# Two decoder blocks on one core: norms, scale, turning and splitting by row tile at the experts' end, and turnings placed among early products

## The chip, the cores and the metric

The kernel runs on one core of one Trainium2 chip. The metric is the device time of one execution in microseconds (us), given as the median of several runs; smaller is better. The matrix engine is PE (TensorE), the elementwise engines are DVE (VectorE), ACT (ScalarE) and POOL (GpSimd), and SP (SyncE) issues most DMAs. PE's clock has two levels, 2.4 GHz (granted clock 1.00 in the profile) and 1.2 GHz (0.50).

## The reference, cut to what matters

Two blocks of a language model work one after the other on 512 tokens of width 1024, all in float32.

```python
for l in range(2):                                    # block one
    p = x @ w_in[l]                                   # four mixers follow
    h = layer_norm(ALPHA * h + mix, ln1_g, ln1_b)
    f = swiglu(h, ...) if l == 0 else moe(h, ...)     # 8 experts, top 2
    h = layer_norm(ALPHA * h + f, ln2_g[l], ln2_b[l])
# block two: x is block one's h
x = x + 0.5 * rms_norm(swiglu(rms_norm(x, ffn1_pre_g), ...), ffn1_post_g)
y = hybrid_mixer(rms_norm(x, mix_pre_g), ...)
x = x + rms_norm(y, mix_post_g)
x = x + 0.5 * rms_norm(swiglu(rms_norm(x, ffn2_pre_g), ...), ffn2_post_g)
```

Between block one's experts and block two's first feed-forward stand a layer norm, a root-mean-square norm with the gain `ffn1_pre_g`, and nothing else.

## The kernel before

Tokens are four row tiles (t = 0 to 3) of 128 tokens; features are eight tiles of 128. A float32 product is made of three products of rounded parts: every operand is split into a rounded part (ACT copies it) and a rest (DVE subtracts), so one "unit" of a feed-forward (128 gate and 128 up columns for 512 tokens) is 48 matmuls of 512 columns, and a projection piece of 256 columns is 48 as well. The layer's input must lie with features on the partitions, in `XR` (`x_split`): PE transposes it ("turns" it) into PSUM, ACT copies the rounded part, DVE subtracts for the rest.

The program is a row of stages, each a `Block` in which every engine has its own list of instructions; all engines meet at a stage's end. Inside, engines wait only for semaphore counts. The order on each engine is the order in which it is written.

- **Start.** `stage_load` (L2688 to L2704) loads the input `x` in one DMA, then constants, then the first two weight pieces, and waits for the inputs. `stage_to_feature` (L2725 to L2744) turns all 32 tiles, ACT and DVE split them by feature tile. `stage_stream` then splits piece 0 (ACT L2864, DVE L2884) and multiplies (PE L2847).
- **Experts.** `stage_moe` loops over eight experts. Its DVE function `end` (L3881, L3887) adds the last expert rows, which POOL gathers by indirect DMA (L3712) after ACT has stored them. Then come five stages: `stage_layer_norm` (DVE L3289 to L3301, ACT's early rounding of the next gate/up unit L219), `stage_begin_two` (a copy, L3907), `stage_pre_norm` (ACT squares L3944, L3949, DVE L3957), `stage_to_feature` (PE L2725, ACT L2733, DVE L2744, and the rest of the early unit, DVE L225), `stage_ffn` (PE L2506 to L2508).
- **Ends of other stages.** A tail (`MixOut`, `LayerTail`, `RootTail`, `OutTail`) norms row tile by row tile, and PE turns each tile (`pe_turn`; L2194 in `MixOut`, L1784 in the others). As soon as tiles 0 and 1 are split, a `HeadStart` lets PE multiply the next stage's first unit or piece for those 256 tokens (`pe_first_tokens`, L242, 48 matmuls of 256 columns); the next stage opens with the other 256 tokens (`pe_last_tokens`, L242 too). In `MixOut` and `LayerTail` all 48 stand ahead of the turning of tile 3; in `RootTail` and `OutTail` tile 2 is turned first, then come the 48, then tile 3.

## Time and profile before

| what | us |
|---|---|
| median of 3 runs (2971.95 to 2977.4) | 2974.25 |
| the profiled execution | 2977.13 |
| its span, first to last instruction | 2975.3 |
| PE busy | 2775.5 (93%) |
| DVE busy | 1543.2 (52%) |
| ACT busy | 1086.0 (37%) |
| POOL busy | 208.2 (7%) |

The span is 1.8 us shorter than the execution; the rest lies before the first and after the last instruction. PE is the busiest engine by far. A matmul's printed time overlaps with its neighbours' (512 columns are printed as 390 ns and follow each other every 227 ns), so the starts of rows are the better ruler. "Idle before" in a row is the time for which the engine had nothing to do, and what ended it.

### The profile page before, as it was taken

What the parts mean: (1) busy time and instruction counts of PE and PEld (TensorE: products, weight loads), DVE (VectorE), ACT (ScalarE), POOL (GpSimd) and SP (SyncE); (2) the same over time, 40 slices, a digit from 0 to 9 for tenths busy, and PEclk for the clock granted to TensorE, in tenths of its full rate; (3) what the DMA queues carried; (4) which work ended last, traced back from release to release, by engine and by line L of the source; (5) the groups of instructions that cost most, each with busy time, mean ns of one, the idle gap of its engine ahead of it and who ended that gap; (6) DMA issues with size and microseconds to landing.
All of it is one profiled execution on the core that took longest, in us unless ns stands there. A gap on an engine that the chain in (4) does not pass through costs nothing. (4 is left out here: it accounts for less than half of the span.)

```text
span 2975.3 us, 38798 instructions
## 1 busy us (share of the span) xinstructions
PE 2775.5 (93%) x14972; PEld 2386.3 (80%) x14972; DVE 1543.2 (52%) x2136; ACT 1086.0 (37%) x1524; POOL 208.2 (7%) x205
## 2 busy tenths in 40 slices
PE   7999999999999999969999999949999997899999
PEld 5778888888877798858988888848888775788887
DVE  3526675233355366647777777773232525742433
ACT  2434223222233242235555565532232416531222
POOL 0011200000000122050000000110000002000000
PEclk9998889999999999979999999979999996899999
DMA  4210024143222100248888888954242120251521
GB/s 152 90 62 1 29 71 124 50 138 85 85 83 90 45 1 29 86 123 235 250 237 234 228 236 235 271 144 113 60 135 85 54 64 20 85 142 50 149 69 66
DMA packets 435566, 335.25 MB, mean 113 GB/s; under 512 B 23488, under 2 KB 375744, under 8 KB 435312
## 3 DMA queue, kind: packets, MB, share of 16 engines
q1 hardware_dynamic: 429360, 318.14, 37.2%
q0 software_dynamic: 3008, 10.09, 1.0%
q10 hardware_dynamic: 3072, 5.24, 0.5%
q8 instruction: 91, 1.49, 0.2%
q14 instruction: 35, 0.29, 0.0%
HBM read 323.43 MB, written 9.99 MB: 112 GB/s over the span
## 5 line engine op out<-in xcount | busy, mean ns | idle before, releaser
L2506 PE MATMUL psum<-x_split,gate_up_split 128*128 128x512 f32 x1024 | 399.2, 390 | 2.1 <-PEq L2715 2.1
L2507 PE MATMUL psum<-x_split,gate_up_split 128*128 128x512 f32 x1024 | 399.0, 390 | 0.0
L2508 PE MATMUL psum<-x_split,gate_up_split 128*128 128x512 f32 x1024 | 398.9, 390 | 0.0
L3586 PE MATMUL psum<-x_slots_split,gate_up_split 128*128 128x320 f32 x1424 | 381.1, 346 | 16.4 <-DVE gate_up_split L3807 12.9
L3587 PE MATMUL psum<-x_slots_split,gate_up_split 128*128 128x160 f32 x1424 | 315.9, 242 | 0.0
L2634 DVE TENSOR_TENSOR arena<-arena,psum 128x512 f32<-128x512 f32 x66 | 45.4, 688 | 488.1 <-ACT arena L2572 488.1
L2847 PE MATMUL psum<-x_split,w_split 128*128 128x512 f32 x1152 | 271.9, 395 | 12.0 <-DVE w_split L2884 6.8
L3586 PEld LDWEIGHTS psum<-x_slots_split,gate_up_split 128*128 128x128 f32 x1424 | 262.6, 190 | 24.6 <-issue 22.6
L2847 PEld LDWEIGHTS psum<-x_split,w_split 128*128 128x128 f32 x1152 | 217.0, 190 | 66.6 <-issue 14.5
L3587 PEld LDWEIGHTS psum<-x_slots_split,gate_up_split 128*128 128x128 f32 x1424 | 266.1, 192 | 1.9
L2572 ACT ACTIVATE arena<-psum 128x512 f32<-128x512 f32 x66 | 39.6, 601 | 594.9 <-PE psum L2508 594.9
L2506 PEld LDWEIGHTS psum<-x_split,gate_up_split 128*128 128x128 f32 x1024 | 192.5, 188 | 42.3 <-issue 2.3
L2508 PEld LDWEIGHTS psum<-x_split,gate_up_split 128*128 128x128 f32 x1024 | 192.6, 188 | 40.1
L2507 PEld LDWEIGHTS psum<-x_split,gate_up_split 128*128 128x128 f32 x1024 | 192.6, 188 | 39.8
L3807 DVE TENSOR_TENSOR gate_up_split<-arena,gate_up_split 128x2048 fp32r<-128x2048 f32 x88 | 201.0, 2284 | 0.0
L2602 DVE TENSOR_TENSOR gate_up_split<-arena,gate_up_split 128x2048 fp32r<-128x2048 f32 x63 | 144.4, 2292 | 75.9 <-ACT gate_up_split L2553 75.9
L2525 PE MATMUL psum<-down_split,hidden_split 128*128 128x512 f32 x432 | 168.6, 390 | 1.1 <-DVE hidden_split L2636 1.1
L2526 PE MATMUL psum<-down_split,hidden_split 128*128 128x512 f32 x432 | 168.1, 389 | 0.0
L2527 PE MATMUL psum<-down_split,hidden_split 128*128 128x512 f32 x432 | 168.1, 389 | 0.0
L3740 ACT ACTIVATE gate_up_split<-arena 128x2048 fp32r<-128x2048 f32 x88 | 167.4, 1903 | 0.0
L3812 DVE TENSOR_TENSOR down_split<-arena,down_split 128x512 fp32r<-128x512 f32 x176 | 121.2, 692 | 70.6 <-ACT down_split L3746 70.0
L2847 PE MATMUL psum<-w_split,x_split 128*128 128x512 f32 (+1 forms) x672 | 143.0, 374 | 2.1 <-PE psum L2847 2.1
(520 smaller groups left out, 4790.2 us busy)
## 6 DMA issues: line engine op xcount, KB each, us to landing
arena<-in_moe_w_gate SPq DMA_DIRECT2D x91, 512.0 KB, 4.2
arena<-in_moe_w_up SPq DMA_DIRECT2D x91, 512.0 KB, 5.6
arena<-in_moe_w_down SPq DMA_DIRECT2D x176, 256.0 KB, 5.1
arena<-in_ffn_w_gu SPq DMA_DIRECT2D x88, 512.0 KB, 5.3
arena<-in_w_in SPq DMA_DIRECT2D x32, 1024.0 KB, 5.2
arena<-in_ffn_w_down SPq DMA_DIRECT2D x108, 256.0 KB, 5.2
arena<-in_ffn_w_gate SPq DMA_DIRECT2D x22, 512.0 KB, 4.1
arena<-in_ffn_w_up SPq DMA_DIRECT2D x22, 512.0 KB, 5.6
```

What stands on the lines that cost most here:

```text
L2506: nc.tensor.matmul(out, w[0], XR[:, 0, k, :], start=k == 0, stop=False)
L2507: nc.tensor.matmul(out, w[0], XR[:, 1, k, :], start=False, stop=False)
L2508: mm = nc.tensor.matmul(out, w[1], XR[:, 0, k, :], start=False, stop=k == DT - 1)
L2525: nc.tensor.matmul(out, x[0], w[0], start=f == 0, stop=False)
L2526: nc.tensor.matmul(out, x[0], w[1], start=False, stop=False)
L2527: mm = nc.tensor.matmul(out, x[1], w[0], start=False, stop=f == FU - 1)
L2602: nc.vector.tensor_tensor(GSPL[:, r, 1, :], GRAW[:, r, :], GSPL[:, r, 0, :].bitcast(F32), ALU.subtract).then_inc(*g_lo.up())
L2847: mm = nc.tensor.matmul(out, a, b, start=opens and k == 0 and q == 0, stop=closes and k == nk - 1 and q == 2)
L3586: hi = lambda start, stop: nc.tensor.matmul(out, wt[0], XE[:, k8, :, :].rearrange("p s n -> p (s n)"), start=start, stop=stop)
L3587: lo = lambda: nc.tensor.matmul(out[:, N:2 * N], wt[1], XE[:, k8, 0, :], start=False, stop=False)
L3740: nc.scalar.activation(GSPL[:, r, 0, :], GRAW[:, r, :], ACT.Copy).then_inc(g_hi.sem, 1)
L3807: nc.vector.tensor_tensor(GSPL[:, r, 1, :], GRAW[:, r, :], GSPL[:, r, 0, :].bitcast(F32), ALU.subtract).then_inc(g_lo.sem, 1)
```

## The change

- **Start** (`stage_begin` in place of two stages): the constants with the identity matrix are loaded first, then weight piece 0, then `x` in four DMAs, one for each row tile, then piece 1 and the rest. Each tile is turned as it comes; ACT and DVE split piece 0 and then the tiles; PE multiplies piece 0 for the first 256 tokens around the turning of tile 3. The projection of layer 0 then opens with the last 256 tokens.
- **Experts' end** (`MoeTail`, inside `stage_moe`): five stages go. DVE computes the norm statistics between the last additions of expert rows; the norms, the scale (the gain is now a row, multiplied in on DVE), the turning and the splitting go two row tiles at a time; PE multiplies the next unit for tiles 0 and 1 in between. SP loads the next gate/up units as soon as the last expert's are split, then three rows; POOL computes the rest of the early unit.
- **Other ends**: `pe_first_tokens` is cut up, and the turnings stand among its products. In `RootTail` and `OutTail`, DVE splits tile 1's rests before it scales tile 2.

```diff
+    def pool_rest(self):
+        nc.gpsimd.tensor_tensor(self.split[:, 1], self.raw, self.split[:, 0].bitcast(F32), ALU.subtract)...
+class MoeTail(Part):
+    def sp_tail(self):
+        self.early.sp_load()
+        sp.dma_start(self.G, self.rows[0].partition_broadcast(P)).then_inc(*self.gain_in.up(16))
+        sp.dma_start(k.PAR[:, 0:64], k.ap["par2"]).then_inc(*self.par_in.up(16))
+        sp.wait_ge(*self.left.at(1))
+        for r, to in zip(self.rows[1:], (self.Bb, self.pre)):
+            sp.dma_start(to, r.partition_broadcast(P)).then_inc(*self.rows_in.up(16))
...
+    def pe_tail(self):
+        self.pe_turn(0)
+        self.pe_turn(1)
+        self.start.pe_ready(self.moved.at(4), self.parts.at(4))
+        self.start.pe_first_tokens(0)
+        self.start.pe_first_tokens(1)
+        self.pe_turn(2)
+        self.pe_turn(3)
...
+    def dve_norm(self, t):
+        s.link(nc.vector.bn_aggr(self.mv[:, t, :], self.st[:, t, :]))
+        nc.vector.tensor_scalar(self.col(self.rs, t), ..., LN_EPS, None, ALU.add)
+        s(nc.vector.scalar_tensor_tensor(y, y, self.mv[:, t, 0:1], self.G, ALU.subtract, ALU.mult))
+        nc.vector.wait_ge(*self.root.at(t + 1))
+        s.link(nc.vector.reciprocal(self.col(self.rs, t), self.col(self.rs, t)))
+        nc.vector.scalar_tensor_tensor(self.X2[:, t, :], y, self.col(self.rs, t), self.Bb, ...)
...
+    def dve_tail(self):
+        for t in (0, 2):
+            self.dve_norm(t)
+            self.dve_norm(t + 1)
+            self.dve_scale(t)
+            self.dve_scale(t + 1)
+            self.dve_rests(t)
+            self.dve_rests(t + 1)
...
     def pe_end(self):                                  # RowTail, used by LayerTail
+        start.pe_first_tokens(0)
+        start.pe_first_tokens(1, range(0, DT // 2))
+        self.pe_turn(TT - 1)
+        start.pe_first_tokens(1, range(DT // 2, DT))
...
+    def pe_end(self):                                  # RootTail and OutTail
+        start.pe_first_tokens(0)
+        self.pe_turn(TT - 2)
+        self.pe_turn(TT - 1)
+        start.pe_first_tokens(1)
...
+                sp.dma_start(self.CF[:, :], ap["const_f"]).then_inc(*const_in.up(16))
+                early.sp_load()
+                for t in range(TT):
+                    sp.dma_start(H[:, t, :], ap["x"][0, t * P:(t + 1) * P, :]).then_inc(*rows_in[t].up(16))
+                early.second(sp)
...
+                            if i == 1:
+                                wait(dve, b, high_used, 2 * TT, TT + t)
+                                nc.vector.bn_stats(tail.st[:, t, 0:6], H[:, t, 0:HALF])
                             wait(dve, b, high_in[i][t], 16, 16)
                             nc.vector.scalar_tensor_tensor(y, YHIGH[:, i, t, :], ..., y, ALU.mult, ALU.add)
+                            if i == 1:
+                                wait(dve, b, high_used, 2 * TT, TT + t + 1)
+                                nc.vector.bn_stats(tail.st[:, t, 6:12], y)
```

PE at the program's start, before. `h_tok` is the input by tokens, `w_split` a split weight piece:

```order
L2721 UNCONDITIONAL_BRANCH
L2725 MATMUL psum<-const_sb,h_tok 128x128 x32
L2715 UNCONDITIONAL_BRANCH
L2822 UNCONDITIONAL_BRANCH
L2847 MATMUL psum<-x_split,w_split_59 128x512 x48
```

And now, where `w_split_early` is piece 0:

```order
L2869 UNCONDITIONAL_BRANCH
L2876 MATMUL psum<-const_sb,h_tok 128x128 x24
L246 MATMUL psum<-x_split,w_split_early 128x256 x24
L2876 MATMUL psum<-const_sb,h_tok 128x128 x8
L246 MATMUL psum<-x_split,w_split_early 128x256 x24
L2856 UNCONDITIONAL_BRANCH
L2978 UNCONDITIONAL_BRANCH
L246 MATMUL psum<-x_split,w_split_early 128x256 x48
L3003 MATMUL psum<-x_split,w_split_60 128x512 x48
```

Half of piece 0's products moved ahead of the stage's end, and the last eight turnings stand among them.

DVE at the experts' end, before: the additions of expert rows, the statistics and the norm, in two stages:

```order
L3881 SCALAR_TENSOR_TENSOR h_tok<-keep,small,h_tok 128x1024 x4
L3505 ISA x2
L3887 SCALAR_TENSOR_TENSOR h_tok<-arena,small,h_tok 128x512 x8
...
L3289 BN_STATS arena<-h_tok 128x6 x8
L3292 BN_AGGR arena<-arena 128x2 x4
L3294 TENSOR_SCALAR arena<-arena 128x4
L3297 SCALAR_TENSOR_TENSOR h_tok<-h_tok,arena 128x1024 x4
L3299 RECIPROCAL arena<-arena 128x4
L3301 SCALAR_TENSOR_TENSOR h_tok<-h_tok,arena 128x1024 x4
```

And now, up to the second of the four last additions:

```order
L4001 SCALAR_TENSOR_TENSOR h_tok<-keep,small,h_tok 128x1024 x4
L3616 ISA x2
L4010 SCALAR_TENSOR_TENSOR h_tok<-arena,small,h_tok 128x512 x4
L3616 ISA
L4008 BN_STATS arena<-h_tok 128x6
L4010 SCALAR_TENSOR_TENSOR h_tok<-arena,small,h_tok 128x512
L3616 REGISTER_ALU
L4013 BN_STATS arena<-h_tok 128x6
L4008 BN_STATS arena<-h_tok 128x6
L4010 SCALAR_TENSOR_TENSOR h_tok<-arena,small,h_tok 128x512
```

The eight statistics moved from behind the additions to between the last four.

PE at the end of block two's first feed-forward (`RootTail`), before, and then now; `down_tail_split` is the last product of that stage:

```order
L1772 MATMUL psum<-down_tail_split,hidden_split 128x512
L1784 MATMUL psum<-const_sb,h_tok 128x128 x16
L242 MATMUL psum<-x_split,w_split_early 128x256 x48
L1784 MATMUL psum<-const_sb,h_tok 128x128 x8
L2444 UNCONDITIONAL_BRANCH
L2822 UNCONDITIONAL_BRANCH
L242 MATMUL psum<-x_split,w_split_early 128x256 x48
```

```order
L1919 MATMUL psum<-down_tail_split,hidden_split 128x512
L1931 MATMUL psum<-const_sb,h_tok 128x128 x8
L246 MATMUL psum<-x_split,w_split_early 128x256 x24
L1931 MATMUL psum<-const_sb,h_tok 128x128 x16
L246 MATMUL psum<-x_split,w_split_early 128x256 x24
L2607 UNCONDITIONAL_BRANCH
L2978 UNCONDITIONAL_BRANCH
L246 MATMUL psum<-x_split,w_split_early 128x256 x48
```

Products now stand behind the last turning, where nothing stood before.

## Rows read from the trace of the kernel before

**Rows 1.** Windows: span, PE, PEld, DVE, ACT, POOL busy us, PEclk, DMA share, GB/s.
```profile
1950.00:2000.00 50.00, 11.69 (x48) 10.43 (x49) 36.51 (x46) 17.39 (x23) 4.52 (x4) 0.56 0.40 108
```

**Rows 2.** Timeline of PE, experts' end: start us, us, engine line operation [idle before].
```profile
1986.25 6.56 PE L2725 MATMUL psum<-const_sb,h_tok 128*128 128x128 f32 x32 [37.21 <-PEq L3940]
1994.86 0.47 PE L2506 MATMUL psum<-x_split,gate_up_split 128*128 128x512 f32 x1 [2.05 <-PEq L2715]
```

**Rows 3.** Timeline of ACT, experts' end: one square, and the first unit's SiLU.
```profile
1978.74 1.06 ACT L3944 ACTIVATE h_tok<-keep 128x1024 f32<-128x1024 f32 x1 [5.07 <-PEq L3899]
...
2007.66 0.60 ACT L2572 ACTIVATE arena<-psum 128x512 f32<-128x512 f32 x1 [2.34 <-PE psum L2508]
```

**Rows 4.** Timeline of DVE, experts' end.
```profile
1951.32 2.74 DVE L3887 SCALAR_TENSOR_TENSOR h_tok<-arena,small,h_tok 128x512 f32<-128x512 f32 x4
...
1958.81 0.75 DVE L3887 SCALAR_TENSOR_TENSOR h_tok<-arena,small,h_tok 128x512 f32<-128x512 f32 x1 [0.73 <-DMA arena<-expert_rows,arena]
1960.51 4.85 DVE L3289 BATCH_NORM_STATS2 arena<-h_tok 128x6 f32<-128x512 f32 x8 [0.95 <-PEq L3514]
```

**Rows 5.** Timeline of POOL, experts' end: the last of the four last gathers.
```profile
1955.18 0.95 POOL L3712 DMA_INDIRECT arena<-expert_rows,arena  x1 [0.30 <-issue]
```

**Rows 6.** Line L3712, the gathers at the experts' end, no weights loading beside.
```profile
DMA to landing us min/median/max: 3.4/3.6/5.5
```

**Rows 7.** Line L3704, earlier gathers, SP's weight loads running beside.
```profile
DMA to landing us min/median/max: 4.0/6.0/7.6
```

**Rows 8.** Timeline of POOL, block two's mixers.
```profile
2489.57 4.51 POOL L1418 TENSOR_TENSOR arena<-arena 128x2048 f32<-128x2048 f32 x1 [16.85 <-ACT arena L1466]
```

**Rows 9.** Timeline of DVE, there: the same small operation twice.
```profile
2493.02 1.08 DVE L1661 TENSOR_TENSOR arena<-arena 128x4 f32<-128x4 f32 x1 [8.81 <-ACT arena L1647]
...
2503.18 0.16 DVE L1661 TENSOR_TENSOR arena<-arena 128x4 f32<-128x4 f32 x1
```

**Rows 10.** Timeline of DVE, LayerTail's end: norm of tile 3, then rests.
```profile
832.58 0.21 DVE L1835 BATCH_NORM_AGGREGATE arena<-arena 128x2 f32<-128x12 f32 x1
...
835.61 1.28 DVE L1803 TENSOR_TENSOR x_split<-psum,x_split 128x512 fp32r<-128x512 f32 x2
838.82 1.29 DVE L1803 TENSOR_TENSOR x_split<-psum,x_split 128x512 fp32r<-128x512 f32 x2 [1.93 <-ACT x_split L1797]
```

**Rows 11.** Timeline of PE, LayerTail's end and the next stage's opening.
```profile
831.72 6.00 PE L242 MATMUL psum<-x_split,w_split_early 128*128 128x256 f32 x48
837.56 1.03 PE L1784 MATMUL psum<-const_sb,h_tok 128*128 128x128 f32 x8
840.43 7.47 PE L242 MATMUL psum<-x_split,w_split_early 128*128 128x256 f32 x48 [1.84 <-PEq L2444]
```

**Rows 12.** Window in that opening: columns as in rows 1.
```profile
842.00:844.00 2.00, 2.00 (x11) 2.00 (x11) 1.64 (x1) 0.33 (x1) 0.00 (x0) 0.50 0.96 317
```

**Rows 13.** Timeline of PE, RootTail's end and the next stage's opening.
```profile
2362.24 1.94 PE L1784 MATMUL psum<-const_sb,h_tok 128*128 128x128 f32 x8 [3.77 <-DVE h_tok L1957]
2364.21 7.49 PE L242 MATMUL psum<-x_split,w_split_early 128*128 128x256 f32 x48
...
2374.41 5.99 PE L242 MATMUL psum<-x_split,w_split_early 128*128 128x256 f32 x48 [1.84 <-PEq L2444]
```

**Rows 14.** Timeline of DVE, RootTail's end: the scale of tile 2.
```profile
2361.35 1.41 DVE L1957 SCALAR_TENSOR_TENSOR h_tok<-keep,arena 128x512 f32<-128x512 f32 x2
```

**Rows 15.** Timeline of all engines, the program's start.
```profile
13.11 5.01 PE L2725 MATMUL psum<-const_sb,h_tok 128*128 128x128 f32 x32 [13.11 <-PEq L2688]
...
20.55 3.71 ACT L2864 ACTIVATE w_split<-arena 128x2048 fp32r<-128x2048 f32 x2 [1.56 <-PEq L2715]
22.50 4.49 DVE L2884 TENSOR_TENSOR w_split<-arena,w_split 128x2048 fp32r<-128x2048 f32 x2 [2.24 <-ACT w_split L2864]
...
24.93 13.31 PE L2847 MATMUL psum<-x_split,w_split 128*128 128x512 f32 x48 [6.81 <-DVE w_split L2884]
```

**Rows 16.** Windows at the start: columns as in rows 1.
```profile
4.00:6.00 2.00, 0.00 (x0) 0.00 (x0) 0.00 (x0) 0.00 (x0) 0.00 (x0) 1.00 1.00 399
```

More of the change, by code:

```diff
@@ L1787, in pe_end @@
     def pe_end(self):
-        for t in range(TT - self.behind, TT):
-            if t == TT - 1 and self.start is not None:
-                self.start.pe_first_tokens(self.moved.at(4), self.bank_free())
-            self.pe_turn(t)
+        start = self.start
+        start.pe_ready(self.moved.at(4), self.bank_free())
+        start.pe_first_tokens(0)
+        start.pe_first_tokens(1, range(0, DT // 2))
+        self.pe_turn(TT - 1)
+        start.pe_first_tokens(1, range(DT // 2, DT))
     def act_turned(self, t):
@@ L2681, in tok, with stage_begin @@
         return self.area(TOK0, TT, TOKW)[:, :, col:col + n]
-    def stage_load(self, ahead):
-        nc, ap = self.nc, self.ap
-        loaded = self.sig("inputs_loaded")
+    def stage_begin(self, early, start):
+        nc, ap, XR, H = self.nc, self.ap, self.XR, self.H
+        rows_in = [self.sig(f"x_rows_loaded{t}") for t in range(TT)]
+        const_in, loaded, turned, parts, moved = (self.sig(n) for n in ("identity_loaded", "inputs_loaded", "turned_to_feature", "feature_tile_split", "feature_tile_copied"))
+        bank = lambda t, b: self.bank(2 * t + b)
+        part = lambda i, t, b: XR[:, i, b * (DT // 2):(b + 1) * (DT // 2), t * P:(t + 1) * P]
+        tile = lambda t, b: bank(t, b).rearrange("p (k n) -> p k n", n=P)
         with nc.Block() as block:
@@ L2920, in shift @@
             return ft(u[1]), self.par(l, "mu", i), self.SM[:, OWN_MU + 9 * l + i:OWN_MU + 9 * l + i + 1]
-        self.stage_stream(w, pieces, units, HT0, copy_out, row=row, shift=shift, beside=beside, ring=PSPL if l is None else IN_RING, banks=banks, early=0 if l == 0 else 1, start=start)
+        self.stage_stream(w, pieces, units, HT0, copy_out, row=row, shift=shift, beside=beside, ring=PSPL if l is None else IN_RING, banks=banks, early=1, start=start)
     def rotary_beside(self):
@@ L3369, in beside @@
                     rotary(eng, p)
-            self.project(ap["w_in"][l], IN_PIECES, IN_UNITS, rows[l * 5 + 4], self.ft, self.tok, l=l, beside=beside, start=self.piece_start() if l > 0 else None)
+            self.project(ap["w_in"][l], IN_PIECES, IN_UNITS, rows[l * 5 + 4], self.ft, self.tok, l=l, beside=beside, start=self.piece_start())
             if l == 0:
@@ L3550, in _ @@
                         body(b * E + e, e, 0, 0)
+                        for c in (g_hi, g_lo):
+                            wait(sp, b * E + e, c, FU, nth(FRING - 2) + 1 + FU)
+                            sp.sem_inc(raw_free.sem, 1)
+                tail.sp_tail()
             @block.tensor
```

303 lines of the change are left out of this document (156 added, 147 removed).

## Prediction

> **What bounds the kernel now.** I first read the page's busy times: PE is at 93%, so the question is where its other 7% lies and which engine holds it there. The windows answer: in 1950 to 2000 us PE is busy for 11.69 of 50 us while DVE works 36.51 [rows 1]. The timelines show why. PE has nothing for 37.21 us before it turns the tiles at 1986.25, and the next unit's first product starts at 1994.86 [rows 2], while DVE adds expert rows, takes statistics, norms, copies and scales in a row [rows 4]. The same picture, smaller, stands at the program's start, where PE turns 32 tiles from 13.11 to 18.1 and then waits until 24.93 for DVE's rests of piece 0 [rows 15], and at four stage ends, where PE turns the last tile, then waits 1.84 us for ACT, DVE and the stage's change [rows 11, 13]. Elsewhere PE is full, so time taken from these places should reach the end.
>
> **Experts' end.** Time T0 is when DVE may begin the norms. Four additions of the last group of rows end at 1951.32 + 2.74 = 1954.06, each 0.69 us; the eight statistics take 4.85 / 8 = 0.61 each [rows 4]. Put between the last four additions they make 4 x 0.69 + 8 x 0.61 = 7.6 us, until 1961.7, if rows come in time; before, the last addition started at 1958.81. Leaving the loop takes up to the 0.95 us seen ahead of the statistics [rows 4]: T0 = 1962.6.
>
> POOL now also computes the rest of the early unit, 128x2048. It can start when the last gather is issued, 1955.18 + 0.95 = 1956.1 [rows 5], and a tensor_tensor of that size took 4.51 [rows 8], until 1960.6. Beside that one, a DVE operation of 128x4 with two inputs in SBUF took 1.08 us instead of 0.16 and ended at 2494.10, when POOL's did (2489.57 + 4.51 = 2494.08) [rows 8, 9]. The additions of expert rows have two inputs in SBUF as well. So the second one, due at 1956.6, waits until 1960.6, and then 3 x 0.69 + 5 x 0.61 = 5.1 us follow: 1965.7, and T0 = 1966.6. I take this value, since it rests on the nearest row. The Trainium skill says the same against this change, in "SBUF — State Buffer", section "SBUF: two separate sides": a DVE operation with two SBUF inputs and a GpSimd operation that reads SBUF exclude each other for the whole instruction. The trace agrees with it in rows 8 and 9. Without that rule T0 would be 1962.6.
>
> SP now loads 2 MB of weights from about 1945 and three rows (1.5 MB) behind them, in the time of the last gathers. Gathers landed after a median 3.6 us alone and 6.0 beside weight loads [rows 6, 7]. If all come 2.4 us later, the first addition also falls behind POOL's start: 1960.6 + 4 x 0.69 + 7 x 0.61 = 1967.7, and T0 = 1968.6. This is the far bound. The near one is 1962.6. DVE's other new wait, for the three rows, has nothing else queued before it and should be over by 1962; ACT's rounding of the early unit (some 2 us) and PE's one small turning that tells SP that the hidden area is free lie in idle time.
>
> From T0, for two row tiles: a norm takes 835.61 - 832.58 = 3.03 [rows 10], two 6.1. DVE then waits for the square of the second tile on ACT, 1.06 [rows 3], with its sum and root some 1.5. Scaling in two halves takes 1.4 [rows 14] and a reciprocal 0.25, 1.65, for the second tile 2.0 with its root. Four rests take 2 x 1.28 = 2.6 [rows 10]; PE's turning at the low clock (6.56 / 8 = 0.82 for four [rows 2]) runs beside the scaling. The sum is 13.8, and 27.5 for both pairs, with 0.3 for the stage's change 27.8. The next stage opens at 1966.6 + 27.8 = 1994.4, against 1994.86: nearly all that the stages saved goes into smaller pieces, waits for ACT and the lock. What is won is the work already done: of the first unit only 48 matmuls of 256 columns remain, 5.99 to 7.47 us [rows 11, 13], say 6.7, where the unit took until 2007.66 - 0.2 [rows 3]. The new end is 2001.1: **6.4 us** won, 10.4 at T0 = 1962.6 (11.1 with 6.0 for the rest), 3.7 in the worst pair (T0 = 1968.6 and 7.47). The next unit's split (1.9 on ACT, 2.3 on DVE) is ready 4.4 us into the stage, under the 6.7.
>
> **Start.** Before, DMA moved 399 GB/s once it ran [rows 16]. Constants and piece 0 (1.1 MB) should be there at about 6 us, x tiles (0.5 MB each) at 7.4, 8.7, 10.0. ACT rounds piece 0 in 1.86, DVE's rest takes 2.25 [rows 15]: 10.3. Four rests of tiles 0 and 1, 2.6, follow: 12.9. PE then has 24 products (3.0), eight turnings (5.01 / 4 = 1.25), 24 products (3.0), and 0.3 for the change: 20.4. Some of it will run at 1.2 GHz, since PE has worked little before; before the change the first products behind such a gap took 13.31 us [rows 15] where 48 full ones, 227 ns apart, take 10.9. I take 21.0. The last 256 tokens need 6.7: piece 0 is done at 27.7, against 24.93 + 13.31 = 38.24: **10.5 us**. Bounds: 12 with the high clock throughout; 8 if DMAs land 1 us late and the low clock holds for most of the first products. Piece 1's split is ready at 21.0 + 4.4 = 25.4, in time. SP's later loads all move up with the stage.
>
> **Other ends.** In LayerTail and MixOut the products and the turning of tile 3 fill 831.72 to 837.56 + 0.8; the stage could end 0.5 later, 838.9, instead of opening the next at 840.43 [rows 11]: 1.4 us. DVE's two last rests (1.29 [rows 10]), 1.3 us earlier too, now end beside the products. Moreover PE idles 1.84 us there now, and the clock stood at 0.50 in the window at 842 [rows 12], so the next 48 took 7.47 and not 5.99: 1.5 us more, which I expect to go since the gap goes. In RootTail and OutTail PE starts when tile 1's rests are done, 2361.35 + 1.28 = 2362.65 [rows 14, 10], instead of turning tile 2 at 2362.24; the same work and the last turning, 9.8 us, ends at 2372.5, and the next stage opens 0.5 later, 2372.9, instead of 2374.41 [rows 13]: 1.5 us. The sum is 2 x 2.9 + 2 x 1.5 = **8.8 us**; 5.8 if the clock falls all the same, 3 if DVE is late besides, 9.5 at best.
>
> **Sum.** 6.4 + 10.5 + 8.8 = 25.7. The profiled execution took 2977.13 us, which gives 2951.4; the median of the runs is 2.9 lower, so I forecast **2948.5 us**. The bounds add up to 14.7 and 32.6 won, 2959.6 and 2941.7. With the scatter of the runs the range is 2940 to 2961.
>
> **Rivals.**
> - *No lock*: POOL's subtraction doesn't hold DVE, T0 = 1962.6, won 4 more: 2944.5. Against it stands the 1.08 us [rows 9]; for it, that one small operation is thin evidence and that POOL may come late.
> - *Late rows and a falling clock*: gathers 2.4 us late (T0 = 1968.6) and the clock still falls at the two ends and in the first unit: 2 + 3 + 0.8 less, 2954.3.
> - *The start doesn't pay*: x tiles queue behind piece 0's many short packets, or ACT and DVE are late so that PE stands after tile 2. Half of the 10.5 goes: 2953.8; with the previous rival 2959.6.
> - *Slower than before*: chopped PE work keeps the clock low. At each of six places PE would do 96 products of 256 columns and some turnings at 1.2 GHz; the window at 0.50 holds 11 products in 2 us, 0.18 each [rows 12], against 6.00 / 48 = 0.125 [rows 11], so 96 lose 5.5 us and the turnings beside them some 0.8. Six places lose 38, and the kernel ends near 2974.3 - 25.7 + 38 = 2986.6. It decides from the fifth such place on (25.7 / 6.3 = 4.1). RootTail speaks against it: after 3.77 us idle the 48 products took 7.49 and the next 48 5.99 [rows 13], so the clock comes back within the first.
> - *The change doesn't do what it says*: products stand ahead of the stage's end, but DVE's rests set that end in all cases; then only the start and the halves count, about 14 us: 2960.
>
> **Chances.** Forecast (2944 to 2953) 0.56; no lock 0.14; late rows and clock 0.13; weak start, or rests that set the end, 0.10; no change within 0.2% 0.03; slower 0.04. A measurement of this kernel can tell about 0.2% (6 us) from nothing. Faster by more: 0.93; within 0.2%: 0.03; slower: 0.04.
>
> **What would show it.** At the start: PE's first products at 13 us, the last-token products at 21, piece 1 at 27.7. At the experts' end: one addition that starts at 1956.6 less what the start won and lasts 4 us longer than 0.69; last addition at about 1965 on the old scale; rests of tile 3 at 27 us behind the first aggregate. At the four ends: gaps of under 0.6 us before the next stage's first product, 48 products in 6.0. Wrong would be: a first addition that waits for its DMA until 1960, products at the experts' end before 1976 on the old scale, a project stage that waits for pieces 1 or 2.

## The result, and the profile after

The changed kernel takes 2950.16 us (median of 12 runs, 2938.68 to 2963.12), beside 2974.77 of the kernel before (12 runs). The ratio is 0.9922, with a 95% interval of 0.9904 to 0.994. In a second series of six runs, beside two of the experiments, it was 2938.64 us, ratio 0.9895 (0.987 to 0.9919). The forecast was 2948.5. Faster, and by what was said; but one of its three terms was not won at all, and stretches that the change doesn't touch came out 3.7 us shorter in its trace. The single run of all experiments that fell into a slow state (3899.69 us at a granted clock of 0.65, of "The rest on DVE") is left out of every number below. The profiled execution took 2954.24 us, 22.9 less than the profiled one of before.

I followed marks that exist in both traces and noted how much earlier each comes in the new one. The difference grows or shrinks only where something was won or lost.

| stretch | offset behind it | won | forecast |
|---|---|---|---|
| start, to piece 1's first product | 11.6 | 11.6 | 10.5 |
| unchanged work until MixOut turns tile 2 | 17.4 | 5.8 | 0 |
| MixOut's end | 20.3 | 2.9 | 2.9 |
| LayerTail's end | 23.3 | 2.9 | 2.9 |
| unchanged work until the experts' row additions | 19.75 | -3.5 | 0 |
| experts' end, to the next part's unit 1 | 19.2 | -0.5 | 6.4 |
| RootTail's end | 21.2 | 2.0 | 1.5 |
| unchanged work until OutTail's end | 22.7 | 1.4 | 0 |
| OutTail's end | 23.0 | 0.3 | 1.5 |

**The start**, timeline of PE in the profile of after, answering rows 15:

```profile
13.48 3.10 PE L246 MATMUL psum<-x_split,w_split_early 128*128 128x256 f32 x24 [0.36 <-DVE x_split L2902]
16.43 1.03 PE L2876 MATMUL psum<-const_sb,h_tok 128*128 128x128 f32 x8
17.22 3.12 PE L246 MATMUL psum<-x_split,w_split_early 128*128 128x256 f32 x24
20.63 5.98 PE L246 MATMUL psum<-x_split,w_split_early 128*128 128x256 f32 x48 [0.30 <-PEq L2856]
```

Piece 1 follows at 26.91, where it followed at 38.54. The first 24 products took 3.10 us, the time of the high clock, right behind 24 turnings.

**LayerTail's and OutTail's ends**, timeline of PE, answering rows 11 and 13:

```profile
811.38 4.55 PE L246 MATMUL psum<-x_split,w_split_early 128*128 128x256 f32 x36
...
818.65 5.98 PE L246 MATMUL psum<-x_split,w_split_early 128*128 128x256 f32 x48 [0.40 <-PEq L2607]
```

```profile
2580.67 5.46 PE L246 MATMUL psum<-x_split,gate_up_split 128*128 128x256 f32 x24 [4.54 <-DVE x_split L1952]
2585.93 2.15 PE L1931 MATMUL psum<-const_sb,h_tok 128*128 128x128 f32 x16
2587.83 3.12 PE L246 MATMUL psum<-x_split,gate_up_split 128*128 128x256 f32 x24
2591.25 5.98 PE L246 MATMUL psum<-x_split,gate_up_split 128*128 128x256 f32 x48 [0.30 <-PEq L4159]
```

The gap ahead of the next stage is 0.3 to 0.4 us in place of 1.84, and the last 48 products take 5.98 and not 7.47. In OutTail the gap at the end goes too, but PE idles 4.54 us for tile 1's rests at the front, where it idled 3.89 before, and comes out of it at the low clock (granted clock 0.50 from 2581 to 2585 us; 5.46 us for 24 products against 3.12 a moment later).

**The experts' end**, answering rows 2, 4 and 5. SP, ACT and POOL:

```profile
1925.81 5.76 SPq L2548 DMA_DIRECT2D arena<-in_ffn_w_gu  x4
1931.61 2.43 SPq L294 DMA_DIRECT2D arena<-in_rows  x1
```

```profile
1926.90 0.38 ACTq L3881 DMA_DIRECT2D expert_rows<-arena  x1
1948.03 1.91 ACT L219 ACTIVATE gate_up_split<-arena 128x2048 fp32r<-128x2048 f32 x1 [21.60 <-DVE h_tok L4010]
1949.96 1.28 ACT L332 ACT_TABLE_LOAD   x1
```

```profile
1934.22 0.94 POOL L3829 DMA_INDIRECT arena<-expert_rows,arena  x1 [6.76 <-DMA expert_rows<-arena]
...
1950.03 4.50 POOL L224 TENSOR_TENSOR gate_up_split<-arena,gate_up_split 128x2048 fp32r<-128x2048 f32 x1 [11.11 <-ACT gate_up_split L219]
```

DVE and PE in the same stretch:

```profile
1941.13 0.75 DVE L4010 SCALAR_TENSOR_TENSOR h_tok<-arena,small,h_tok 128x512 f32<-128x512 f32 x1 [5.43 <-DMA arena<-expert_rows,arena]
...
1948.44 0.19 DVE L368 BATCH_NORM_AGGREGATE arena<-arena 128x2 f32<-128x12 f32 x1
...
1951.58 0.16 DVE L372 RECIPROCAL arena<-arena 128x1 f32<-128x1 f32 x1 [1.57 <-ACT arena L336]
1951.78 3.82 DVE L373 SCALAR_TENSOR_TENSOR keep<-h_tok,arena 128x1024 f32<-128x1024 f32 x1
...
1957.21 1.29 DVE L373 SCALAR_TENSOR_TENSOR keep<-h_tok,arena 128x1024 f32<-128x1024 f32 x1
```

```profile
1966.34 5.99 PE L246 MATMUL psum<-x_split,gate_up_split 128*128 128x256 f32 x48 [1.61 <-DVE x_split L389]
...
1979.84 8.55 PE L246 MATMUL psum<-x_split,gate_up_split 128*128 128x256 f32 x48 [1.69 <-PEq L3625]
```

The row of POOL before the change that the first of these answers, and the landing of its last four gathers (rows 6 has all eight):

```profile
1950.70 1.31 POOL L3712 DMA_INDIRECT arena<-expert_rows,arena  x1 [3.50 <-DMA expert_rows<-arena]
```

```profile
DMA to landing us min/median/max: 3.4/3.6/3.6
```

Three waits took the place of what the stages had cost. POOL waits 6.76 us for the last expert's store, where it waited 3.50, and the four last gathers then land 6.4 to 7.2 us after issue instead of 3.4 to 3.6 (the line of after stands below, under "A version that beats both"). ACT's wait for the last addition, written at the end of its pass, holds back the rounding of the next unit and the table load, so that DVE stands 1.57 us before L372. And POOL's rest, behind that rounding, lies exactly on the first tile's L373: 3.82 us for what takes 1.29 for the next tile.

### The profile page after: what moved, and what is told of

It is laid out like the page before. It is cut to its first block and busy times, and to the rows that moved or that the text cites. A ratio compares the mean times of both kernels' runs of the same rounds, so it can differ in the third digit from the quotient of the medians.

```text
span 2952.4 us, 38976 instructions
## 1 busy us (share of the span) xinstructions
PE 2765.6 (94%) x15069; PEld 2382.1 (81%) x15069; DVE 1544.3 (52%) x2152; ACT 1083.0 (37%) x1529; POOL 212.7 (7%) x206
## 5 line engine op out<-in xcount | busy, mean ns | idle before, releaser
L2669 PE MATMUL psum<-x_split,gate_up_split 128*128 128x512 f32 x1008 | 392.2, 389 | 0.0
L2670 PE MATMUL psum<-x_split,gate_up_split 128*128 128x512 f32 x1008 | 392.1, 389 | 0.0
L2671 PE MATMUL psum<-x_split,gate_up_split 128*128 128x512 f32 x1008 | 392.1, 389 | 0.0
L3003 PE MATMUL psum<-x_split,w_split 128*128 128x512 f32 x1104 | 257.1, 392 | 5.2 <-PE psum L3003 4.3
L3003 PEld LDWEIGHTS psum<-x_split,w_split 128*128 128x128 f32 x1104 | 205.4, 188 | 56.5 <-issue 14.3
L2671 PEld LDWEIGHTS psum<-x_split,gate_up_split 128*128 128x128 f32 x1008 | 189.2, 188 | 39.6
L2669 PEld LDWEIGHTS psum<-x_split,gate_up_split 128*128 128x128 f32 x1008 | 189.2, 188 | 39.1
L2670 PEld LDWEIGHTS psum<-x_split,gate_up_split 128*128 128x128 f32 x1008 | 189.2, 188 | 39.0
```

Source lines behind the costliest of these rows:

```text
L2669: nc.tensor.matmul(out, w[0], XR[:, 0, k, :], start=k == 0, stop=False)
L2670: nc.tensor.matmul(out, w[0], XR[:, 1, k, :], start=False, stop=False)
L2671: mm = nc.tensor.matmul(out, w[1], XR[:, 0, k, :], start=False, stop=k == DT - 1)
L3003: mm = nc.tensor.matmul(out, a, b, start=opens and k == 0 and q == 0, stop=closes and k == nk - 1 and q == 2)
```

## Theories

- *Won and not won.* The start and the four ends are worth 11 and 8 us; the new experts' end is worth nothing. Rival: it is worth the forecast 6.4, and the clock hides it.
- *Loads beside the store.* SP's early loads (2 MB of weights and 1.5 MB of rows) hold up the last store and gathers. Rival: ACT or POOL are late by their own work.
- *The lock.* POOL's rest stops a DVE operation with two inputs in SBUF wherever it lies. Rival: L373 is slow for a reason of its own.
- *The clock.* The unforeseen 5.8 and -3.5 us are the granted clock's. Rival: the change reaches stretches that I took for unchanged.

For the experts' end I use one length in all kernels: from the first addition of expert rows (L3881 before, L4001 after) to the first product of the next part's unit 1. It is 61.15 us before and 61.67 after.

## Experiments on the parts

**The start alone.** The kernel before, with the new first stage. The whole of its edit in the calling code:

```diff
-        self.stage_load(self.first_pieces(ap["w_in"][0], IN_PIECES, HT0))
-        self.stage_to_feature(self.H, None, split=self.XR)
+        self.stage_begin(self.early_piece(ap["w_in"][0], IN_PIECES), self.piece_start())
```

> The kernel before with the new start alone (turning by row tile, unit 1's products among the turnings); the experts' end and the four other ends are as before. The forecast put the start at 10.5 us, and the mark in the trace of after (the first product of piece 1 at 26.91 against 38.54) shows 11.6. Theory: the whole kernel is 10 to 12.5 us shorter, a ratio of 0.9958 to 0.9966, and that mark stands at 26.9. Rival (what is won at the start is lost again in the work behind it, since engine and clock are the limit there): the mark at 26.9, but the time within 4 us of before.

Measured: 2963.86 us (5 runs), ratio 0.9953 (0.9924 to 0.9983); piece 1 starts at 27.77. That is 11.1 us at the median, 5 to 23 by the interval, so what is won at the start stays won; the rival's 4 us lie just outside. The mark is 0.9 us later than the 26.9 expected: the first rows of `x` were there at 8.82 us and not at 7.99. In the other traces with this start it stands between 26.9 and 27.4.

**The other ends alone.** The kernel before, with the new order in its four ends:

```diff
-        for t in range(TT - self.behind, TT):
-            if t == TT - 1 and self.start is not None:
-                self.start.pe_first_tokens(self.moved.at(4), self.bank_free())
-            self.pe_turn(t)
+        start.pe_first_tokens(0)
+        start.pe_first_tokens(1, range(0, DT // 2))
+        self.pe_turn(TT - 1)
+        start.pe_first_tokens(1, range(DT // 2, DT))
```

> The kernel before with the new order of turnings and next unit's products at the four other ends alone (MixOut, LayerTail, and the first two feed-forward and output ends of the root layer). The forecast's term is 8.8 us (2.9, 2.9, 1.5, 1.5). Theory, from the marks of after (2.9, 2.9, 2.0, 0.3): 8.1 us shorter, a ratio near 0.9973. Rival (marks are exact, but a higher granted clock gave part of them): 5 to 6 us, the order alone without the clock's share.

Measured: 2967.17 us (10 runs), ratio 0.996 (0.9939 to 0.9981), 7.8 us by the medians. In its trace the last 48 products of LayerTail's end took 5.99 us behind a gap of 0.41, with the clock as forecast. By the same marks as in the table its four ends won 2.9, 2.8, 1.4 and 0.3 us, 7.4 in all. The interval is too wide to tell 8.1 from the 5 to 6 of the rival; the marks lie nearer to 8, and RootTail's 1.4 is lower than the 2.0 of after because its first 24 products took 5.20 us and not 4.60.

**All but the experts' end.** The changed kernel with `stage_layer_norm`, `stage_begin_two`, `stage_pre_norm` and the turning stage back in their places. These are the four stages that the change removes; the fifth one counted with them, `stage_ffn`, stays in both and only opens with other products.

```diff
-                               [rows[7], rows[8], rows[16]], self.swiglu_unit(ap["ffn1_w_gu_2"][0]), self.unit_start((0, 1)))
+        self.first_of_two = self.swiglu_unit(ap["ffn1_w_gu_2"][0])
+        self.stage_layer_norm(rows[7], rows[8], early=self.first_of_two)
```

> The changed kernel with the experts' end of before: norm, transfer and turning in their own stages. Theory (the new experts' end is worth nothing, as the marks say: unit 1's first product of the next part came 0.5 us later by the offset than before the experts' end): the time of after within 2 us, 2950, ratio 0.991 to 0.993. Rival (the new end is worth the 6.4 us of the forecast, and the marks hide it behind a lower clock): 2956 to 2957, ratio 0.994.

> The changed kernel with the experts' end of before, once more, since four runs left it open on which side of after it lies. Theory (the new end is worth nothing or costs 1 to 3 us, as the stretch from the first addition to the first product of hidden values says: 60.1 us here against 63.6 in after): at or below the time of after, by 0 to 3 us. Rival (worth something): above it.

Measured: 2948.4 us (4 runs), ratio 0.9898 (0.9867 to 0.9929), and in the second series 2951.86 (6 runs), 0.9919 (0.9894 to 0.9943), with 2938.64 for the changed kernel beside it. The second series alone speaks for the rival, the first against it. Over both series the mean of its 10 runs is 2950.4, that of 18 runs of the changed kernel 2947.9, and two standard errors are 5.2 and 4.0: no difference that the runs could show, and 6.4 is neither shown nor quite ruled out by them. The length of the experts' end is sharper. It is 59.3 and 61.4 us in the two traces of this kernel and 61.15 before, with the same code; it is 61.7 and 58.5 in the two traces of the changed kernel. The means are 60.6 and 60.1. Most of the scatter is PE's clock in the last piece of the length: with the old end unit 0's 48 products took 12.6, 11.0 and 12.6 us (before, and the two traces), with the new end the last 48 took 8.55 and 5.98. With the fast value throughout, 11.0 and 5.98, the old end stands at 59.6, 59.3 and 59.8, the new one at 59.1 and 58.5. **The new experts' end is worth about 0.5 us, at most some 1.3**, where I had put 6.4.

**The changed kernel once more.**

> The changed kernel once more, word for word, beside the next two on the same chip, to have the three against each other within about a us. Expected: 2950 us, ratio 0.991 to 0.994. Its trace also gives the stretches of unchanged code a second time (piece 1's first product to the turning of tile 2 at MixOut's end: 424.6 us before, 418.9 in the first trace of after); if the granted clock alone moves them, the same program shows another length here, and the other change of that length has no cause in the change.

Measured: 2938.64 us (6 runs), ratio 0.9895 (0.987 to 0.9919). That is 11 us below the 2950 expected, and each series' ratio lies outside the other's interval. Its trace shows what the same program does twice. DVE's first addition of expert rows, in the first trace and in this one:

```profile
1926.56 4.87 DVE L4001 SCALAR_TENSOR_TENSOR h_tok<-keep,small,h_tok 128x1024 f32<-128x1024 f32 x4
```

```profile
1912.31 4.87 DVE L4001 SCALAR_TENSOR_TENSOR h_tok<-keep,small,h_tok 128x1024 f32<-128x1024 f32 x4
```

That is 14.3 us for nothing but another execution. At MixOut's end the last 48 products start at 448.25 and not 453.82, though the start was 0.5 us later. The windows of the stretch, of the kernel before, of after and of after once more (columns as in rows 1):

```profile
40.00:440.00 400.00, 381.72 (x2217) 330.14 (x2216) 217.24 (x285) 128.56 (x164) 47.27 (x41) 0.93 0.17 52
```

```profile
40.00:440.00 400.00, 374.94 (x2227) 324.28 (x2227) 225.32 (x300) 128.59 (x165) 47.97 (x41) 0.95 0.17 52
```

```profile
40.00:440.00 400.00, 376.18 (x2256) 324.84 (x2255) 230.11 (x309) 130.34 (x168) 47.84 (x41) 0.97 0.17 52
```

The granted clock there is 0.93, 0.95 and 0.97, and the matmuls done in 400 us rise with it, 2217, 2227, 2256. From piece 1's first product to the turning of tile 2 the stretch takes 424.65, 418.85 and 412.80 us. The kernel with the other ends alone, which has before's code up to that mark, takes 420.77 there. And from LayerTail's end to the row additions, where the first trace had lost 3.5 us, the second gains 5.2. So neither the 5.8 us nor the -3.5 needs a cause in the change, and the rival falls. This is the theory of the clock, shown as far as it says that executions of one program differ by as much; it was not tried what makes one execution get more of it.

## Experiments on the experts' end

**The loads alone, in the kernel before.** Only SP's place for them is another.

```diff
                     with sp.Fori(E - 1, E) as e:
                         body(b * E + e, e, 0, 0)
+                        for c in (g_hi, g_lo):
+                            wait(sp, b * E + e, c, FU, nth(FRING - 2) + 1 + FU)
+                            sp.sem_inc(raw_free.sem, 1)
+                self.first_of_two.sp_load()
```

> The kernel before; moved is one thing: the loads of the next part's first two units (four of 512 KB on SP's queue) are issued at the end of the experts' stage, behind the last split of the slot they use, and no longer in the norm's stage. Nothing there needs them earlier. Theory (these loads share the DMA engines with ACT's store and POOL's gathers of the last expert and hold them up): from ACT's store to POOL's first gather of the second half 6 to 7.5 us in place of 4.0, the last addition of gathered rows 4 to 8 us later behind the end of the experts' products than in the kernel before, and the time up by as much, less what the norm's stage no longer waits for; ratio 1.001 to 1.002. Rival (POOL's own work or ACT's late start is the cause, the loads none): the store and gathers as in the kernel before within 1 us, ratio 1.000 or just below.

Measured: 2977.83 us (10 runs), ratio 1.0004 (0.9989 to 1.0019). POOL and DVE:

```profile
1948.27 1.24 POOL L3714 DMA_INDIRECT arena<-expert_rows,arena  x1 [5.76 <-DMA expert_rows<-arena]
```

```profile
1953.67 2.09 DVE L3889 SCALAR_TENSOR_TENSOR h_tok<-arena,small,h_tok 128x512 f32<-128x512 f32 x3 [3.47 <-DMA arena<-expert_rows,arena]
1956.15 0.75 DVE L3889 SCALAR_TENSOR_TENSOR h_tok<-arena,small,h_tok 128x512 f32<-128x512 f32 x1 [0.40 <-DMA arena<-expert_rows,arena]
```

The wait for the store is 5.76 us in place of 3.50, the last addition comes 14.55 us after the first of the pass in place of 12.51, and the whole length is 62.9 in place of 61.15. So 2 MB on SP's queue cost 1.8 to 2 us of the chain, with the loads' place alone changed. From ACT's store to POOL's first gather it is 6.3 us, as the theory had it (6 to 7.5), so the rival falls; but the last addition is 2 us later and not 4 to 8, and the ratio 1.0004 shows no loss. The whole time can't show 2 us.

**The unit's loads held back.** In the changed kernel POOL reports when the last gathered rows have landed, and SP waits for it:

```diff
     def sp_tail(self):
-        self.early.sp_load()
         sp.dma_start(self.G, self.rows[0].partition_broadcast(P)).then_inc(*self.gain_in.up(16))
...
+        sp.wait_ge(*self.landed.at(1))
+        self.early.sp_load()
```

> The changed kernel; SP issues the loads of the next part's two units (2 MB) and of the small parameters only when the gathered rows of the last half have landed; the three rows of gains stay ahead. Theory (the loads hold up the store and the gathers): the gap from the store to POOL's first gather back to 4 to 5 us, the last addition 4 to 7 us earlier by the offset; the rounding of the unit comes later by the loads' 5 to 8 us, but is needed only by the first products, so that the experts' end is 3 to 6 us shorter than in after, 2944 to 2947. Rival (the loads only move to where they are late): the additions earlier as said, but the first 48 products and the rounding later by as much, time equal to after within 1 us. Second rival (loads not the cause): gap still over 6.5 us.

Measured: 2947.81 us (4 runs), ratio 0.9927 (0.9907 to 0.9947). POOL, DVE and ACT:

```profile
1922.91 0.94 POOL L3831 DMA_INDIRECT arena<-expert_rows,arena  x1 [5.52 <-DMA expert_rows<-arena]
```

```profile
1932.72 0.73 DVE L4013 SCALAR_TENSOR_TENSOR h_tok<-arena,small,h_tok 128x512 f32<-128x512 f32 x1
...
1940.10 0.16 DVE L374 RECIPROCAL arena<-arena 128x1 f32<-128x1 f32 x1 [4.43 <-ACT arena L338]
1940.30 3.82 DVE L375 SCALAR_TENSOR_TENSOR keep<-h_tok,arena 128x1024 f32<-128x1024 f32 x1
```

The gathers land 3.7 to 3.9 us after issue, and the last addition comes 16.2 us after the first of the pass, where it was 20.5 in after: 4.3 us. Three of them go again. ACT rounds the late unit before it takes the first root, so DVE waits 4.43 us for the root and not 1.57. The length is 58.8 us. The theory holds for the gathers and the additions, and so does half of its rival: the load became late at its new place, through ACT's order, and of the 3 to 6 us 1.4 are left (4.3 less 2.9). It fails for the store: from its issue to POOL's first gather it is 6.06 us, where 4 to 5 were expected. POOL still waits 5.52, with the three gain rows (1.5 MB) beside the store; that these rows are the reason was not tried alone. The whole times (2941 to 2959) show no difference from the changed kernel.

Once the trace had shown transfers slowing each other, the Trainium skill, "DMA: Bandwidth & Descriptors", section "Issuing engines are not separate DMA queues", had the reason: DMAs from ACT, SP and GpSimd run on the same engines and interleave. The runs agree and give the price, which the page doesn't.

**ACT's wait moved.** The wait for a pass's additions stands at the start of the next pass:

```diff
-                def end(b):
-                    act.wait_ge(high_used.sem, high_used.base + b * (2 * TT) + 2 * TT)
+                def begin(b):
+                    wait(act, b, high_used, 2 * TT, 0)
```

> The changed kernel; ACT's wait for all additions of a pass stands at the start of the next pass and no longer at the end of the last one, so that the rounding of the next unit (1.9 us), the table load (1.3) and the first root run while the gathers are under way, and POOL's rest (4.5 us) moves with them. Theory: L372 no longer waits 1.57 us for the root, and the norm L373 takes 1.3 in place of 3.8, since POOL's rest lies elsewhere; its 2.5 us are paid in the additions only if it falls on one. 1.5 to 4 us shorter than after: 2946 to 2949. Rival (POOL's rest is paid wherever it lies, and ACT's work delays the store): no shorter than after by more than 0.5 us.

Measured: 2946.27 us (4 runs), ratio 0.9894 (0.9854 to 0.9935). POOL and DVE:

```profile
1947.23 4.51 POOL L224 TENSOR_TENSOR gate_up_split<-arena,gate_up_split 128x2048 fp32r<-128x2048 f32 x1
```

```profile
1948.78 3.52 DVE L4011 SCALAR_TENSOR_TENSOR h_tok<-arena,small,h_tok 128x512 f32<-128x512 f32 x1 [4.56 <-DMA arena<-expert_rows,arena]
...
1953.54 0.73 DVE L4011 SCALAR_TENSOR_TENSOR h_tok<-arena,small,h_tok 128x512 f32<-128x512 f32 x1
...
1960.36 0.15 DVE L372 RECIPROCAL arena<-arena 128x1 f32<-128x1 f32 x1
1960.55 1.29 DVE L373 SCALAR_TENSOR_TENSOR keep<-h_tok,arena 128x1024 f32<-128x1024 f32 x1
```

POOL's rest moved forward, and the slow operation with it. L373 is back at 1.29, and the first of the last additions takes 3.52 us instead of 0.73; it ends at 1952.3, POOL at 1951.7. That is the lock as the prediction drew it, on an addition, and it is paid there: the last addition comes 22.5 us after the first, not 20.5. The wait for the root is gone. The length is 58.0 us, with its last 48 products at 7.48; what is gained is 2 to 2.6 us at equal clock, as the theory had it. The four runs (2932 to 2960) can't show that.

**The rest on DVE.**

```diff
             self.dve_norm(t + 1)
+            if t == 0:
+                self.early.dve_rest(here=True)
             self.dve_scale(t)
...
-                tail.pool_tail()
```

> The changed kernel; the rest of the next unit's rounding is worked out by DVE (2.3 us) behind the second tile's norm, where it waits 1.25 us for ACT's square, and no longer by POOL (4.5 us). Theory (POOL's work holds up DVE's two-input operations on SBUF, 2.5 us of it): L373 of the first tile back from 3.82 to 1.28 us, DVE's own work up by 1.0 net, so 1.5 us shorter than after at the end of the additions' norm. Rival (L373 was slow for another reason, its first read of rows that had just landed for one): L373 stays at 3.8, and the end is 1 us later than in after.

Measured: 2950.76 us (median of 3 runs), ratio 0.9914 (0.9896 to 0.9933). DVE:

```profile
1954.39 0.16 DVE L372 RECIPROCAL arena<-arena 128x1 f32<-128x1 f32 x1 [1.57 <-ACT arena L336]
1954.59 1.29 DVE L373 SCALAR_TENSOR_TENSOR keep<-h_tok,arena 128x1024 f32<-128x1024 f32 x1
...
1958.68 2.28 DVE L230 TENSOR_TENSOR gate_up_split<-arena,gate_up_split 128x2048 fp32r<-128x2048 f32 x1
```

With POOL silent and all else in place, L373 takes 1.29 us; the rival falls. The wait for the root, 1.57, stays, as it should. DVE's 2.28 us lie partly in its wait for ACT's square, which was 1.25 and is 0.27 now. The length is 56.4 us, of which 0.8 come from additions that ended that much earlier: POOL waited 6.13 us for the store here and not 6.76, which this edit doesn't explain. The whole time shows none of this within its interval.

## The lengths side by side

All in us from the first addition of expert rows in the trace named; the third column is the next part's last 48 products, which tell the clock.

| kernel | last addition | unit 1's first product | last 48 products |
|---|---|---|---|
| before | 12.5 | 61.15 | - |
| loads alone, in before | 14.6 | 62.9 | - |
| all but the experts' end, two traces | 12.5, 12.5 | 59.3, 61.4 | - |
| changed kernel, two traces | 20.5, 20.5 | 61.7, 58.5 | 8.55, 5.98 |
| unit's loads held back | 16.2 | 58.8 | 7.47 |
| ACT's wait moved | 22.5 | 58.0 | 7.48 |
| the rest on DVE | 19.7 | 56.4 | 5.99 |
| the version below, two traces | 14.8, 14.5 | 50.5, 50.6 | 7.48, 7.44 |

With the last products put at 5.98 throughout, the changed kernel stands at 59.1 and 58.5, held loads at 57.3, ACT's wait at 56.5, the rest on DVE at 56.4, and the version below at 49.0 and 49.1. Traces of one kernel still differ by up to 0.6 us so, and each of the three experiments in between has a single one. A last addition later than before is no loss in itself, since the new kernels take seven statistics ahead of it (0.6 us each).

## A version that beats both

The three findings together, and more: unit 0's load goes out as soon as its slot is free, some 8 us before the last store; the gain row of the first norm is there before the experts' loop; the second unit, the third row and the parameters wait for the landed rows; and in the second pair of tiles ACT takes the third tile's root before it squares the fourth.

```diff
+            if t == 2:
+                self.act_new_root(t)
             self.act_square(t + 1)
-            self.act_new_root(t)
+            if t == 0:
+                self.act_new_root(t)
...
     def sp_tail(self):
+        self.early.first(sp)
+        sp.wait_ge(*self.left.at(1))
+        sp.dma_start(self.Bb, self.rows[1].partition_broadcast(P)).then_inc(*self.rows_in.up(16))
+        sp.wait_ge(*self.landed.at(1))
+        sp.dma_start(self.pre, self.rows[2].partition_broadcast(P)).then_inc(*self.pre_in.up(16))
+        self.early.second(sp)
```

> The changed kernel with what the theories ask for together: the gain row is loaded before the experts' loop, the next part's unit 0 as soon as its slot is free (some 8 us before the last store), its unit 1, the third row and the parameters behind the landed rows; ACT rounds and loads its table while the gathers run; the rest of the rounding is DVE's in its wait for the square; and in the second pair of tiles ACT takes the root of the third tile's sum before it squares the fourth. Theory: store to gather 4 to 5 us (after 7.3), last addition 5 to 7 us earlier, no wait of 1.57 before L372 and no L373 over 1.5 us, 1.25 us less in the second pair, and the first 48 products of the next unit at full clock since PE idles less (2.5): 9 to 13 us shorter than after, 2937 to 2941. Rival (only the additions move, the rest of the end is bound by PE and clock): 4 to 6 us shorter, 2944 to 2946. Second rival (the early load of unit 0 holds up the down weights of the last expert): the loop's end later by 1 us or more.

> The version with held loads, ACT's early work, the rest on DVE and the third tile's root ahead of the fourth's square, once more. Its first trace has that stretch at 53.9 us against 63.6 in after. Theory: 10 us shorter than after, 2938 to 2942. Rival (the first result, 2935.8, was helped by the clock, and most of the 10 us is given back in the next stage, which now starts with a lower clock): 2944 to 2947.

Measured: 2935.81 us (5 runs), ratio 0.9861 (0.9843 to 0.9879), and 2939.21 (6 runs), 0.9874 (0.9849 to 0.99). SP, POOL, DVE and PE of the second trace:

```profile
1919.53 1.00 SPq L2555 DMA_DIRECT2D arena<-in_ffn_w_gu  x2
```

```profile
1932.47 1.08 POOL L3841 DMA_INDIRECT arena<-expert_rows,arena  x1 [3.73 <-DMA expert_rows<-arena]
```

```profile
1942.37 0.73 DVE L4023 SCALAR_TENSOR_TENSOR h_tok<-arena,small,h_tok 128x512 f32<-128x512 f32 x1
...
1945.43 1.28 DVE L377 SCALAR_TENSOR_TENSOR keep<-h_tok,arena 128x1024 f32<-128x1024 f32 x1
```

```profile
1971.17 7.44 PE L246 MATMUL psum<-x_split,gate_up_split 128*128 128x256 f32 x48 [1.69 <-PEq L3636]
1978.45 0.40 PE L2679 MATMUL psum<-x_split,gate_up_split 128*128 128x512 f32 x1
```

The store takes what it took before the change, and the landing of the last four gathers answers it. Line of the gathers, in that stretch, of after and then of this version:

```profile
DMA to landing us min/median/max: 6.4/6.9/7.2
```

```profile
DMA to landing us min/median/max: 3.5/3.6/3.9
```

The length is 50.5 and 50.6 us in the two traces, against 61.7 and 58.5 in the changed kernel and 61.15 before. Counted to the opening of the next stage, where the clock of the last products has no part, it is 43.2 and 43.3 against 53.3 and 52.7. The rows of the second trace beside the first of after say where the 10.0 us are: the norms begin 6.0 earlier, the first pair of tiles is 3.0 shorter (no wait for the root, no lock, DVE's own rest in its place), the second pair with the stage's change 1.0. What each part of the edit gives by itself was not tried. The rivals fall by these lengths: the loss was not PE's and the clock's, and unit 0's early load delays no store (ACT's last two stores are issued 10.4 us apart in all three kernels). Nor is the gain given back in the next stage: from unit 1's first product to RootTail's turning of tile 1 it is 350.0 to 350.1 us in both traces of this version and in both of the changed kernel. The mean of its 11 runs is 2937.3, against 2947.9 of the 18 of the changed kernel, 10.6 us with an uncertainty of some 6.7 (5.4 and 4.0 taken together). That agrees with the 8 to 11 of the traces. The clock's share did not come: the last 48 products took 7.44 us here too.

## Why the prediction was right, and where it was not

- **The time**: right, 2948.5 against 2950.16. Its terms were 10.5, 8.8 and 6.4; the trace shows 11.6, 8.1 and -0.5, which is 19.2, and 3.7 us from stretches that the change doesn't touch. The right number is partly luck: a clock between 0.951 and 0.962 moves the same program from 2963 to 2939, and the sum without its third term, some 2955, would have been inside the range of 2940 to 2961 as well.
- **Start**: right. The products stood at 13.5, the last tokens at 20.6, piece 1 at 26.9 (forecast 13, 21, 27.7). The one wrong part was the allowance for the low clock, 0.8 us; another 0.3 is that piece 1 stood at 38.54 before and not at 38.24, which is the printed end of piece 0.
- **Other ends**: right in sum and at three of them. In MixOut and LayerTail both halves of the term came, 1.4 us of gap and 1.5 of clock. OutTail gave 0.3 of 1.5: its first 24 products, behind a wait of 4.54 us, took 5.46 us, where RootTail's took 4.60 and full speed 3.1, and before the change its 48 had taken 6.81 and not RootTail's 7.49, so that there was less to win. I had worked it out from RootTail alone. Two slips stand in these terms: 840.43 less 838.9 is 1.5 and not 1.4, and by rows 13 RootTail's work with the last turning is 9.3 + 0.8 = 10.1 us and not 9.8, which makes 1.2 of the 1.5.
- **Experts' end: the failed step.** The forecast opened the next stage 48.1 us after the first addition; it was 53.3. Of these 5.2 us the start of the norms (T0, called 1966.6, was 1968.2 on the old scale) is 1.6, the wait for the root 1.6, the lock on L373 2.5, and the pairs themselves gave back 0.5 (the sum has 27.5 for twice 13.8, a slip of 0.1). Two more are the low clock, 8.55 us for the last products where I put 6.7; in the second trace these took 5.98.
  - *Late rows* was among the bounds and not in the sum. I took 2.4 us from the gathers that run beside weights [rows 7], but did not put the store into the same sum; it stands ahead of the gathers and was 3.3 us late itself. The first of the last additions came 6.8 us later than in the sum; one statistic taken ahead of it and a loop left without a pause gave 1.2 back. That T0 was only 1.6 off is luck: 4.0 us of the 1966.6 were the lock on an addition, which didn't come. Against the 1962.6 without it the late rows cost 5.6 us, not the 2.4 of the bound. The rule that was missed: a load that is moved slows each transfer in the chain, not the last alone.
  - *The lock* was right in kind but at another place, because I let ACT's rounding of the unit "lie in idle time". It was smaller too, 2.5 us where 4.0 stood in the sum: DVE's operation stood until POOL's ended, as said, but POOL was 1.75 us into its work when that operation began. ACT's wait at the end of its pass stands in the code ahead of it. Not one addition was held, as the tell-tale said, but the norm. By the Trainium skill, "SBUF — State Buffer", section "SBUF: two separate sides", the lock lasts for the other's whole instruction. The trace agrees: L373 ends at 1955.6, POOL's rest at 1954.5, and the operation had 1.3 us of its own to do, of which it did little before. In the run where the lock met an addition it cost 2.8 us (3.52 for 0.73).
  - *One thing I didn't cost at all*: the table load of 1.28 us ahead of the first root, which the same wait kept until the norms had begun.
- **Rivals**: the falling clock came once in each trace of the experts' end (8.55 us for 48 products in one, 7.46 in the other), not at MixOut's and LayerTail's ends. The slow clock through chopped work did not come: the first products at the start and the last 48 at the four ends ran at full speed (3.10 for 24, 5.98 or 5.99 for 48).

## What to carry to other kernels

When a load is moved to an earlier place, put into the sum every transfer that it now shares the DMA engines with, the stores above all, and hold it back or move it further ahead if one of them is on the chain: here 2 MB at one place cost 2 us in the kernel before and 4.3 us of the additions beside three more rows, and half of it 8 us earlier with the rest behind the landed rows delayed neither the store nor the gathers. When a last stage is merged into a loop, look for waits at the end of the loop's body that only a next pass needs, since they now stand ahead of the tail. And check a right total term by term: here a term of 6.4 us was missing, and the clock had paid 3.7 of it.

## What was not expected of the hardware

The same program met the expert rows' additions at 1912.3 us in one execution and at 1926.6 in another, on the granted clock alone as far as the rows show. 0.8% of the time lies in it (2938.68 to 2963.12 us), as much as the whole change is worth, so that a stretch between two marks tells within 2 us what whole runs leave open. A 4.5 us instruction of POOL cost DVE 2.5 to 2.8 us each time (four traces), on the norm or the addition with two inputs in SBUF that lay beside it. That is 0.2 us less than what was left of POOL's instruction when DVE's began (2.7 to 3.0 us). The small operation of rows 9 fits: it lost 0.9 us, with 1.1 us of POOL's left.
